# Per-kind start offsets for the split weight units in a float32r transformer kernel (one Trainium2 core)

## Time and profile before

| | |
|---|---|
| median of 3 runs | 1498.73 us (1498.37 to 1499.16) |
| profiled execution | 1499.37 us |
| its span, first to last instruction | 1497.5 us |
| PE busy | 1445.4 us (97%), 10475 matmuls |
| PEld busy | 1326.4 us (89%), 10484 weight loads |
| DVE, ACT busy | 930.4 us (62%), 660.1 us (44%) |
| mean granted TensorE clock | 0.987 |

### The profile page before, as it was taken

How to read it: one execution, slowest core, us unless ns; L and a number is a source line. 1 busy time by engine, 2 the same in 40 slices (tenths; PEclk the granted TensorE clock), 3 DMA queues, 4 the chain that set the end, 5 groups by cost and what they waited for, 6 DMA issues and landing times.

```text
span 1497.5 us, 25321 instructions
## 1 busy us (share of the span) xinstructions
PE 1445.4 (97%) x10475; PEld 1326.4 (89%) x10484; DVE 930.4 (62%) x1363; ACT 660.1 (44%) x834; POOL 95.9 (6%) x78
## 2 busy tenths in 40 slices
PE   8989998999999999999999999999999998999997
PEld 6978987899999999999789999999999886799996
DVE  5887457555675555757885555746555767665556
ACT  5655534333444434545244334425334466543342
POOL 0012141000020000100020000100000100100000
PEclk9999998999999999999999999999999999999999
DMA  7443444776568555665356556667555440455551
GB/s 256 150 141 95 146 142 155 219 218 212 193 222 284 185 188 191 198 195 196 113 178 204 187 193 196 198 195 250 179 190 196 147 141 29 141 198 196 196 196 57
DMA packets 191526, 268.43 MB, mean 179 GB/s; under 512 B 5740, under 2 KB 164752, under 8 KB 191182
## 3 DMA queue, kind: packets, MB, share of 16 engines
q1 hardware_dynamic: 186336, 250.05, 51.2%
q0 software_dynamic: 4224, 15.91, 3.2%
q10 hardware_dynamic: 878, 1.21, 0.3%
HBM read 261.92 MB, written 4.19 MB: 178 GB/s over the span
## 4 chain that ended last, share of the span: by engine, by line
PE 84%; DVE 9%; ACT 3%; DMA 2%; issue 1%; POOL 0%; DVEq 0%; ACTq 0%
PE bank L764 82%; DVE split L2024 2%; DMA ring<-in_ffn_w 2%; PE bank L787 2%; ACT split L1553 1%; DVE resid L2101 1%; DVE resid L2109 1%; DVE stats L2080 1%; DVE resid L2078 1%; ACT act_out L1576 0%; DVE arena L2616 0%; DVE stats L2038 0%; DVE arena L2221 0%; ACT gain_rows L1680 0%; DMA resid<-in_x 0%
## 5 line engine op out<-in xcount | busy, mean ns | idle before, releaser
L764 PE MATMUL bank<-hT_hi,split 128*128 128x256 f32 (+1 forms) x3984 | 710.7, 280 | 7.5 <-ACT act_out L1692 5.4
L2024 DVE TENSOR_TENSOR split<-ring,split 128x2048 fp32r<-128x2048 f32 x212 | 484.3, 2286 | 369.1 <-ACT split L1553 363.8
L764 PEld LDWEIGHTS bank<-hT_hi,split 128*128 128x128 f32 (+1 forms) x3984 | 613.8, 189 | 16.0 <-issue 9.8
L1553 ACT ACTIVATE split<-ring 128x2048 fp32r<-128x2048 f32 (+1 forms) x224 | 428.1, 1912 | 352.9 <-PE bank L764 313.7
L764 PE MATMUL bank<-hT_lo,split 128*128 128x256 f32 (+1 forms) x1992 | 556.5, 279 | 0.0
L764 PEld LDWEIGHTS bank<-hT_lo,split 128*128 128x128 f32 (+1 forms) x1992 | 376.3, 189 | 2.0
L764 PE MATMUL bank<-split,hid_hi 128*128 128x512 f32 x992 | 286.2, 395 | 0.0
L764 PEld LDWEIGHTS bank<-split,hid_hi 128*128 128x128 f32 x992 | 183.3, 189 | 37.7 <-issue 0.8
L764 PE MATMUL bank<-split,hT_hi 128*128 128x256 f32 (+1 forms) x896 | 174.1, 294 | 6.5 <-DVE split L2024 4.8
L764 PE MATMUL bank<-split,hid_lo 128*128 128x512 f32 x496 | 158.3, 393 | 0.0
L764 PEld LDWEIGHTS bank<-split,hT_hi 128*128 128x128 f32 x896 | 141.5, 189 | 14.4 <-DVE split L2024 5.4
(11 more groups left out here) (216 smaller groups left out, 964.5 us busy)
## 6 DMA issues: line engine op xcount, KB each, us to landing
ring<-in_ffn_w SPq DMA_DIRECT2D x132, 1024.0 KB, 5.1
ring<-in_w_in SPq DMA_DIRECT2D x19, 1024.0 KB, 5.1
ring<-in_w_mlp_in SPq DMA_DIRECT2D x16, 1024.0 KB, 6.2
ring<-in_w_mlp_out SPq DMA_DIRECT2D x16, 1024.0 KB, 4.9
ring<-in_sgu_w_in SPq DMA_DIRECT2D x16, 1024.0 KB, 5.4
ring<-in_sgu_w_out SPq DMA_DIRECT2D x8, 1024.0 KB, 4.9
ring<-in_kv_w SPq DMA_DIRECT2D x6, 1024.0 KB, 5.4
ring<-in_w_out SPq DMA_DIRECT2D x4, 1024.0 KB, 4.9
```

Source lines behind the costliest of these rows:

```text
L764: ins = pe.matmul(o, lhsT, rhs, start=start, stop=stop)
L1553: act.activation(halves(q if i is None else q + BODY, n)[0], ring[:, u % SLOTS, 0:n], ACT.Copy).then_inc(hi_ready, 1)
L2024: dve.tensor_tensor(lo, ring[:, u % SLOTS, 0:n], hi.bitcast(F32), ALU.subtract).then_inc(split_ready, 1)
```

## The change

A table gives each kind of unit its own offset in elements of 4 bytes: 48 (192 bytes) for all down units in `split`, 32 (128 bytes) for all `mu`, `w1`, `w3` and `su`, none for `sv`. Units by tokens other than `sv` keep 32. Kinds outside the table keep what they had. Units in `two` are not touched.

```diff
+SHIFTS = {"wout": 3 * SHIFT // 2, "md": 3 * SHIFT // 2, "w2": 3 * SHIFT // 2, "so": 3 * SHIFT // 2, "wo": 3 * SHIFT // 2,
+          "mu": SHIFT, "w1": SHIFT, "w3": SHIFT, "sv": 0, "su": SHIFT}
+
+
 def split_shift(q):
 
-    return SHIFT if by_token(SPLIT_NAMES[q]) else 0
+    name = SPLIT_NAMES[q]
+    if by_token(name) and name[0] != "sv":
+        return SHIFT
+    return SHIFTS.get(name[0], 0)
```

## The result

The changed kernel takes 1512.76 us (median of 4 runs, 1507.80 to 1513.43), the kernel before 1498.55 (4 runs, 1493.39 to 1499.16): a ratio of 1.0088, with a 95% interval of 1.0056 to 1.0121. It is slower by 13 us by the ratio, 14 by the medians, where 8.5 us less were forecast. The profiled execution took 1507.80 us, with a span of 1506.1; it is the fastest of the four, so its profile shows less of a loss than the medians do.

A forecast was written before the change was run, and what follows sets the result against it. PE was taken to bound the kernel, by the distance between matmul starts, at a short and a long rate. Terms -9.6 + 1.5 - 0.4 = -8.5 us, from the median 1498.73, gave 1490.2 us; range 1484 to 1509.

The forecast's parts named there:

- What bounds the kernel: Whole kernel: PE busy 97% of the span; the time is how far apart its matmuls start, 113.5 or 117.8 ns.
- Other engines at no cost: ACT and DVE writing at other addresses: no cost, since times with and without an offset match; they keep 1.92 and 2.29 us.
- Up units by features, 192 to 320: FFN 2, MLP, `su` and FFN 0's third pair turn short: 9.6 us gained; other bound 11.9 us lost.
- Down units, 192 to 384: 68 down units: 0.4 us taken as gained, bound 7.0 us in both directions; up units' rates left as they are.
- rival 2: `w1` and `w3` loops of FFN 0, 1 and 3 turn long: 4.1, 8.2 or 11.9 us lost; chance 0.28.
- `sv`, 320 to 192: 342 matmuls of `sv` turn long, as in the second `memkv`: 1.5 us lost, stretching to 40.3 us.
- The rival that addresses mean nothing: All parts keep their rates, the phases being set by stalls ahead of each block: 1498.7 us within 1; chance 0.20.
- Rival 4: Both kinds of up units reach an unseen rate of 109.5 ns a matmul: 29 us gained, 1469 us; chance 0.07.
- The rule of the Trainium skill: PE's weight loads and moving operand have their own read ports, so addresses can't matter between them; the sum would be zero.

The follow-up runs named there:

- S2: Kernel before with down units further by 64 bytes in MLP, 128, 256, 320, 448 in FFN 0 to 3, `su` by 64: 1499.01 us.

## Why the prediction was wrong

- **What bounds the kernel**: right. The time is the distance of PE's matmuls, and it went nowhere else.
- **Other engines at no cost**: right. ACT 1915 and DVE 2293 ns; in FFN 0 ACT waited 51.9 us for PE where it was 54.0.
- **Up units by features, 192 to 320**: this is the step that failed. I took a gain of 9.6 us because units by tokens at 320 ran short. Those have the roles of the operands exchanged, and in the runs the residue 320 is one at which up units behind a down unit were long in all of 18 parts; only `su` and `kv`, behind units by tokens at 320, were short there. The other bound of the same step, a loss of 11.9 us for 29 pairs x 0.41, is what came.
- **Down units, 192 to 384**: failed too. This step priced their own rate alone; what their residue does to the pair behind them was put at nothing in the sum and stood only in rival 2. Their own rate improved by 0.05 us a unit (3.4 us in all, inside the 7.0 of the bound, where I took 0.4), but at 384 they hand the next pair to the long rate, which with the up units left in place cost the pairs of all parts (11 of 11). And "no row at 384" overlooked the down units in `two`, whose residue is the same modulo 256.
- **`sv`, 320 to 192**: right, 40.36 us where 40.3 was written, 1.5 us lost.
- **The rivals**: rival 2 had its place and its price: FFN 0, 1 and 3, 0.41 us a pair, 1512 us for all three. It stood with 0.28, and the range ended at 1509, below its last case. It spoke of a bad entry that may hit one FFN or two; the runs showed an allowed rate that hits all of them. The rival that addresses mean nothing falls with S2. Rival 4 was priced too high: 7.01 us hold two shortened distances at the ends of the block, and in between the 64-column matmuls start 112 ns apart, not 109.5.
- **The rule of the Trainium skill** ("TensorE: Matmul & The Clock Gate", Part 2: the weight load doesn't take read bandwidth from the running matmul): what I drew from it, that addresses can't matter, doesn't hold here. With the same instructions and clock 1.00, the starts were 113.5 to 120.0 ns apart by residue (10.90 to 11.52 us for 96), and the measurement decides. The rule itself isn't refuted by this. I wrote that PE's reads have something to wait for; whether it is the two read streams that collide, or something else that sees the address, no run shows, and neither does any show what it is that locks.
- **One profile as the state of the kernel**: the forecast counted FFN 2 and MLP as long parts to be won. In the repeat they were short in the kernel before. A part of the 9.6 us, up to the 7.5 of these two, wasn't there to be gained in that execution. The sentence that nothing but the turn of the PSUM banks tells FFN 2 from FFN 0 is wrong too: FFN 0 starts with two units by tokens, FFN 2 with units by features between blocks of 64-column matmuls.

**What stays open**: by what mechanism the address acts; why a down unit at 384, the quickest itself, leaves the next pair long; what sets the entry at 192, where 3 parts of 31 were long; and how many residues between the steps of 64 bytes behave otherwise.

## What to carry to other kernels

Where a profile shows the same instructions at two spacings, lay the stretches side by side, and take a second profile before counting on either: it may be a lock that each execution enters anew. Price a change of addresses only from rows with the same operand in the same role and the same form of work ahead of it, since a rate can be handed on by the neighbour. A survey that gives each repeated part of one kernel its own value costs one run for many values.

## What was not expected of the hardware

- The start-to-start distance of a float32r matmul of 256 columns went with the residue of the stationary weights modulo 256 bytes (the moving operand at 128): behind down units 113.5 or 117.8 ns at 192, 118.5 at 0, 117.8 at 64, 120.0 at 128. With 512 columns and moving weights (the stationary operand at 128) it was 229 ns at 192, in some parts 233, 232 at 0, 233 at 64 and 227 at 128.
- One address allows both rates for hundreds of matmuls, by what ran ahead: 384 of `su` took 45.23 us (kernel before) or 43.54 (only the v units moved) at 192, and 45.23 (changed kernel) or 43.53 (only the up units moved) at 320.
- A down unit at 384 turned the next pair from the short to the long rate without a stall between them.
- With one and the same program, MLP and FFN 2 were long in one execution and short in another.
